# Rope products shifted on VectorE and the low parts of a head pair's weights formed on GpSimd, in a latent-attention kernel

## The reference, cut to what matters

```python
q = jnp.einsum('bsr,rhd->bshd', q_c, w_uq)
q_nope, q_rope = q[..., :MLA_NOPE], q[..., MLA_NOPE:]
q_rope = apply_rope(q_rope, cos[:, :, None, :], sin[:, :, None, :])
k_rope = apply_rope(k_r, cos, sin)
...
def apply_rope(x, cos, sin):
    x1 = x[..., :half]; x2 = x[..., half:]
    return jnp.concatenate([x1 * cos - x2 * sin, x2 * cos + x1 * sin], axis=-1)
...
p = softmax over the keys of (q_nope k_nope + q_rope k_rope) * scale, masked
return (o * jax.nn.silu(z)) @ w_out
```

## Time and profile before

| what | value |
|---|---|
| median of 3 runs | 1910.67 us (1909.27 to 1917.45) |
| profiled execution, its own time | 1910.41 us |
| span of its trace | 1908.6 us |
| PE busy | 1826.2 us, 96% of the span |
| DVE, ACT, POOL busy | 43%, 38%, 42% |
| the 8 pairs of heads | 423.3 to 695.6 us |

### The profile page before, as it was taken

One profiled execution on the slowest core, in us unless ns is written; L12 is line 12 of the kernel. 1 busy time (PEld: TensorE's weight loads), 2 busy tenths in 40 slices (PEclk: granted clock), 3 DMA queues, 4 the chain that ended last, 5 costly groups with the idle time before them and its releaser, 6 DMA issues.

```text
span 1908.6 us, 24042 instructions
## 1 busy us (share of the span) xinstructions
PE 1826.2 (96%) x8812; PEld 1504.3 (79%) x8812; DVE 819.2 (43%) x1378; ACT 734.8 (38%) x1022; POOL 802.8 (42%) x998
## 2 busy tenths in 40 slices
PE   5999899989999999899999999999998999999998
PEld 5887778877777778788888888888965788888886
DVE  7478666467666660732151111101668351111102
ACT  2223322264555551422254434322546454344222
POOL 1566565345000044246515555443434135555442
PEclk9999999999999999999999999999999999999999
DMA  9234645421111223233324334332320223333331
GB/s 306 89 111 132 187 155 194 143 62 58 49 58 36 68 89 110 67 88 110 109 68 110 88 101 115 104 110 89 101 70 29 61 73 104 88 106 91 103 107 66
DMA packets 211648, 191.19 MB, mean 100 GB/s; under 512 B 10503, under 2 KB 192890, under 8 KB 211578
## 3 DMA queue, kind: packets, MB, share of 16 engines
q1 hardware_dynamic: 210944, 189.95, 32.2%
q10 hardware_dynamic: 634, 0.29, 0.1%
HBM read 188.12 MB, written 2.10 MB: 100 GB/s over the span
## 4 chain that ended last, share of the span: by engine, by line
PE 79%; DVE 9%; ACT 4%; issue 3%; POOL 2%; DMA 1%; SPq 1%; DVEq 0%; ACTq 0%; POOLq 0%
PE PS L1668 24%; PE PS L1670 24%; PE PS L1669 24%; PE PS L1964 2%; ACT w_high L693 1%; PE PS L1796 1%; POOL w_low L607 1%; DVE soft L1430 1%; ACT probs L870 1%; SPq L433 1%; DVE ada_odd L1085 1%; DMA ada_raw<-in_ada_w 1%; PE PS L1995 1%; POOL w_low L635 1%; DVE q_rope_parts L1417 1%
## 5 line engine op out<-in xcount | busy, mean ns | idle before, releaser
L607 POOL TENSOR_TENSOR w_low<-w_raw,w_high 128x256 fp32r<-128x256 f32 x949 | 741.1, 817 | 1033.1 <-ACT w_high L693 1032.9
L1668 PE MATMUL PS<-h_high,w_high 128*128 128x512 f32 (+1 forms) x1488 | 559.5, 376 | 15.9 <-DVE h_low L1328 7.0
L693 ACT ACTIVATE w_high<-w_raw 128x2048 fp32r<-128x2048 f32 (+1 forms) x150 | 281.9, 1879 | 726.9 <-PE PS L1670 691.4
L1670 PE MATMUL PS<-h_high,w_low 128*128 128x512 f32 (+1 forms) x1488 | 554.7, 373 | 0.0
L1669 PE MATMUL PS<-h_low,w_high 128*128 128x512 f32 (+1 forms) x1488 | 554.7, 373 | 0.0
L1668 PEld LDWEIGHTS PS<-h_high,w_high 128*128 128x128 f32 x1488 | 282.4, 190 | 68.7 <-DVE h_low L1328 8.3
L1670 PEld LDWEIGHTS PS<-h_high,w_low 128*128 128x128 f32 x1488 | 282.2, 190 | 49.1
L1669 PEld LDWEIGHTS PS<-h_low,w_high 128*128 128x128 f32 x1488 | 282.4, 190 | 46.0 <-issue 0.5
L1257 DVE TENSOR_TENSOR w_low<-w_raw,w_high 128x2048 fp32r<-128x2048 f32 x18 | 41.3, 2292 | 338.5 <-ACT w_high L693 338.5
L1202 DVE TENSOR_TENSOR gate_buf<-gate_buf,PS 128x512 f32<-128x512 f32 x44 | 30.3, 688 | 335.0 <-ACT gate_buf L743 334.3
L1668 PE MATMUL PS<-w_high,ff_high 128*128 128x512 f32 x352 | 137.3, 390 | 0.1
(11 more groups left out here) (302 smaller groups left out, 2562.5 us busy)
## 6 DMA issues: line engine op xcount, KB each, us to landing
w_raw<-in_f_gate_up SPq DMA_DIRECT2D x88, 512.0 KB, 4.9
w_raw<-in_e_w_in SPq DMA_DIRECT2D x40, 512.0 KB, 5.1
w_raw<-in_f_down SPq DMA_DIRECT2D x40, 512.0 KB, 4.2
gains<-in_ada_w SPq DMA_DIRECT2D x16, 1024.0 KB, 5.2
w_raw<-in_a_w_in SPq DMA_DIRECT2D x24, 512.0 KB, 4.4
w_raw<-in_o_w_in SPq DMA_DIRECT2D x20, 512.0 KB, 4.4
ada_raw<-in_ada_w SPq DMA_DIRECT2D x8, 1024.0 KB, 11.8
w_raw<-in_e_w_out SPq DMA_DIRECT2D x16, 512.0 KB, 6.5
```

The costliest lines, as they stand in the source:

```text
L607: ins = nc.gpsimd.tensor_tensor(WL[s][:, piece], raw[s][:, piece], WH[s][:, piece].bitcast(F32), ALU.subtract)
L693: nact(WH[s][:, 0:n], raw[s][:, 0:n], ACT.Copy).then_inc(w_high[s], 1)
L1668: mm(dst, lh, rh, start=first, stop=False, skip_group_check=True)
L1670: return mm(dst, ll, rh, start=False, stop=last, skip_group_check=True)
```

## The change

1. **Rope.** TensorE's turn of the rope queries and ScalarE's copy `q_raw` go. VectorE multiplies the rope queries from PSUM by the cosine (128x512), then four blocks of 32 rows from PSUM by the sine, each written to its partner's rows of `q_part`, and adds (`rotated`). The sine table carries the sign of the row that is read (`sign_col`, one more small VectorE instruction while the tables are made). The rope queries of the next pair come right after its queries (`rope_of`), in PSUM bank 4, and their rotation stands at the end of VectorE's pair.
2. **Low parts.** For pairs 1 to 7 GpSimd forms all of slot 0's low part (5 pieces of 256) and columns 768 to 2047 of slot 1's (5 pieces); VectorE forms columns 0 to 767. GpSimd takes slot 0 of pair 1 after `affine`.
3. **Pair order.** `project` holds the keys alone (banks 1 and 5); the values move to after `score(3)`. ScalarE, not VectorE, copies the values out of PSUM. The gates of pair i-1 are multiplied after unit 1 of pair i. The second head's key and rope low parts move behind unit 1. ScalarE writes slot 0's high part at unit 3 (before: unit 0) and the next queries' high part before the Silu. `Z` starts with 4 steps of z, not 3.
4. **Before the first pair** the 4 matmuls of the gate rows go between the third and fourth tile of the latent transposes, and `gate_keep` ahead of `qcL`.

```diff
                 if name == "mla":
...
+                    with pool.Fori(1, 8) as j:
+                        low(j, 0, MLA_CHUNK)
+                        pool.wait_ge(w_high[1], j + (B.split[1] + 1))
+                        for c in range(Z_DVE, CHUNK, SLICE):
+                            piece = slice(c, c + SLICE)
+                            ins = nc.gpsimd.tensor_tensor(WL[1][:, piece], raw[1][:, piece], WH[1][:, piece].bitcast(F32), ALU.subtract)
+                        ins.then_inc(z_pool, 1)
+                        pool.wait_ge(z_pool, j)
+                        pool.wait_ge(z_dve, j)
+                        pool.sem_inc(w_split[1], 1)
+                        pool.sem_inc(raw_free[1], 1)
...
-                act.wait_ge(proj_done, i * 4 + 2)
-                nact(qraw[:, :], PS[:, 0, :], ACT.Copy).then_inc(qa_ready, 1)
                 act.wait_ge(proj_done, i * 4 + 3)
-                nact(knH[:, :, :], PS[:, 4:6, :], ACT.Copy).then_inc(kn_high, 1)
+                for h in range(2):
+                    nact(knH[:, h, :], PS[:, 1 + 4 * h, :], ACT.Copy).then_inc(kn_high, 1)
...
-                    if u == 0:
+                    if u == 2:
+                        act.wait_ge(proj_done, i * 4 + 4)
+                        nact(vh[:, :, :], PS[:, 6:8, :].rearrange("p a (b n) -> p (a b) n", b=2), ACT.Copy).then_inc(kv_ready, 1)
+                    if u == 3:
                         split_high(*(("mla", i + 1) if more else ("oout", 0)), 0)
                 act.wait_ge(used[1], B.use[1] + i + 1)
                 if more:
                     split_high("mla", i + 1, 1)
+                    queries_high(i + 1)
...
+            def rotated(dst, bank):
+
+                v.tensor_tensor(dst[:, :], PS[:, bank, :], cosM[:, :], ALU.mult)
+                half = ROPE // 2
+                for r in range(0, P, half):
+                    to = r + half if r % ROPE == 0 else r - half
+                    ins = v.tensor_tensor(q_part[to:to + half, :], PS[r:r + half, bank, :], sinM[r:r + half, :], ALU.mult)
+                steps.link(ins)
+                return v.tensor_tensor(dst[:, :], dst[:, :], q_part[:, :], ALU.add)
...
                 norm(0)
                 norm(1)
-                v.tensor_copy(vh[:, :, :], PS[:, 6:8, :].rearrange("p a (b n) -> p (a b) n", b=2)).then_inc(kv_ready, 1)
+                keys_low(1)
+                rope_low(1)
+                if not first:
+                    gate_heads(i - 1)
...
                 if more:
-                    split_low("mla", i + 1, 1)
+                    dve.wait_ge(w_high[1], i + (BASE["mla"].split[1] + 2))
+                    v.tensor_tensor(WL[1][:, 0:Z_DVE], raw[1][:, 0:Z_DVE], WH[1][:, 0:Z_DVE].bitcast(F32), ALU.subtract).then_inc(z_dve, 1)
...
+                    rope_queries(i + 1)
...
-                Z = (0, 3, 6, 8, 10, 12, 14, 15, 15, 16, 16)
+                Z = (0, 4, 7, 9, 10, 12, 14, 15, 15, 16, 16)
                 z_parts(0, Z[1])
+                pe.wait_ge(kr_ready, 1)
                 pe.wait_ge(qr_ready, i * 2 + 1)
                 score(0)
+                z_parts(Z[1], Z[1] + 1)
                 pe.wait_ge(qn_ready, i + 1)
                 score(1)
-                z_parts(Z[1], Z[2])
+                z_parts(Z[1] + 1, Z[2])
...
+                    if u == 1:
+                        values_of(i)
...
             with pe.Fori(0, 7) as i:
                 attend(i)
                 queries_of(i + 1)
+                pe.wait_ge(pT_ready, i * 8 + 7)
+                rope_of(i + 1)
                 weigh(i, 1)
                 project(i + 1)
```

More of the change, by code:

```diff
@@ L155, in constants @@
         low = (m % ROPE) < half
-        turn_m[m + half if low else m - half, m] = -1.0 if low else 1.0
+        turn_m[m + half if low else m - half, m] = -1.0
+    sign_col = np.where((r % ROPE) < half, 1.0, -1.0)[:, None].astype(np.float32)
     rot, rh = HD // 4, HD // 8
@@ L895, in attend @@
                 nact(oz[:, 2 * i:2 * i + 2, :], PS[:, 0:2, :], ACT.Silu).then_inc(sz_ready, 1)
-                if more:
-                    queries_high(i + 1)
             queries_high(0)
@@ L1371, in _ @@
                 ins.then_inc(latn_ready, 1)
+            gate_keep(1, 0)
             for j in range(2):
@@ L1377, in _ @@
             ins.then_inc(lat_low, 1)
-            gate_keep(1, 2)
             dve.wait_ge(lat_ev, 4)
@@ L1404, in gate_head, with rope_queries, gate_heads, attend @@
                 v.tensor_tensor(oz[:, i * 2 + h, :], PS[:, 6 + h, :], oz[:, i * 2 + h, :], ALU.mult).then_inc(oz_ready, 1)
-            def attend(i, more):
-                dve.wait_ge(qa_ready, i * 2 + 2)
-                steps.link(v.tensor_tensor(qr[:, :], qraw[:, :], cosM[:, :], ALU.mult))
-                dve.wait_ge(q_turn, i + 1)
-                steps.link(v.tensor_tensor(qraw[:, :], PS[:, 1, :], sinM[:, :], ALU.mult))
-                v.tensor_tensor(qr[:, :], qr[:, :], qraw[:, :], ALU.add).then_inc(qr_sum, 1)
-                dve.wait_ge(kn_high, i + 1)
-                for h, r in enumerate(HEAD_ROWS):
-                    v.tensor_tensor(knL[:, h, :], PS[:, 4 + h, :], knH[:, h, :].bitcast(F32), ALU.subtract)
+            def rope_queries(i):
+                dve.wait_ge(proj_done, i * 4 + 2)
+                rotated(qr, 4).then_inc(qr_sum, 1)
+            def gate_heads(i):
+                dve.wait_ge(sz_ready, i + 1 + CREDIT)
+                gate_head(i, 0)
+                gate_head(i, 1)
+            def attend(i, first, more):
+                def keys_low(h):
+                    dve.wait_ge(kn_high, i * 2 + h + 1)
+                    v.tensor_tensor(knL[:, h, :], PS[:, 1 + 4 * h, :], knH[:, h, :].bitcast(F32), ALU.subtract)
+                def rope_low(h):
+                    r = HEAD_ROWS[h]
                     dve.wait_ge(qr_high, i * 2 + h + 1)
                     v.tensor_tensor(qrHL[HEAD_ROWS[1 - h], h, :], qr[r, :], qrHL[r, h, :].bitcast(F32), ALU.subtract).then_inc(qr_ready, 1)
-                    if h == 0:
-                        v.tensor_tensor(qnL[:, 1, :], PS[:, 3, :], qnH[:, 1, :].bitcast(F32), ALU.subtract).then_inc(qn_ready, 1)
-                dve.wait_ge(proj_done, i * 4 + 4)
-                dve.sem_inc(used[0], 1)
+                keys_low(0)
+                rope_low(0)
+                v.tensor_tensor(qnL[:, 1, :], PS[:, 3, :], qnH[:, 1, :].bitcast(F32), ALU.subtract).then_inc(qn_ready, 1)
                 def top(u):
@@ L1459, in attend @@
                     low_o(1)
-                dve.wait_ge(sz_ready, i + 1 + CREDIT)
-                gate_head(i, 0)
+                    gate_heads(i)
                 if more:
                     queries_low(i + 1)
-                gate_head(i, 1)
+                    rope_queries(i + 1)
             queries_low(0)
-            with dve.Fori(0, 7) as i:
-                steps.loop(i, 2 + 8 * 3)
-                attend(i, True)
+            rope_queries(0)
+            steps.loop(0, 1 + 8 * 3)
+            attend(0, True, True)
+            steps.n = steps.first
+            with dve.Fori(1, 7) as i:
+                steps.loop(i, 1 + 8 * 3)
+                attend(i, False, True)
             steps.done(7)
-            attend(7, False)
+            attend(7, False, False)
             dve.wait_ge(oz_ready, HEADS + CREDIT)
```

49 lines of the change are left out of this document (24 added, 25 removed).

## The result

The changed kernel takes 1904.23 us (median of 7 runs, 1901.73 to 1905.67); the kernel before, run beside it, 1913.01. The measured ratio is 0.9949 with a 95% interval of 0.9934 to 0.9963 (the quotient of the two medians is 0.9954): faster by 0.5%. The profiled execution's span is 1903.4 us, 5.2 less than before.

What follows compares the result with a forecast made beforehand. TensorE, busy 96% of the span, was taken as the bound. Stall +2.2, clock +1.7, steady pairs -10.4 and last pair -0.6 sum to -7.1: 1903.5 us against the median, with an 8-in-10 range of 1897.0 to 1909.5.

Steps and rivals of the forecast that it cites:

- A steady pair without any wait takes 31.12: TensorE in a steady pair: the last pair's 31.99 less the turn's 0.87, so at most 2.5 gained from 33.63.
- The narrow product costs what a wide one does: VectorE's 32-row sine products of the rope queries: 0.69 us each, as fewer rows don't shorten a product.
- The edge costs 0.1: Where one pair meets the next: TensorE's keys wait about 0.1 us for ScalarE's later Silu, with no reserve left.
- Two softmax products lose 0.2 to 0.3 each beside GpSimd, together 0.5: Softmax, around units 6 and 7: GpSimd's slot-0 pieces slow two VectorE products, adding 0.5 us a pair.
- VectorE's chain equals TensorE's: Softmax stretch of a steady pair: VectorE's chain 18.4 us against TensorE's 18.3 of work.
- Five steady pairs: Steady pairs go from 33.63 to 31.9, a gain of 1.73 each; the prediction counted six, 10.4 us.
- Other work before the first pair: net 0: Before the first pair: gate rows fill an idle 1.2, transposes end 0.5 later, `gate_keep` is done sooner; net 0.
- The second pair starts 2.2 later: Second pair's start: TensorE idles 3.8 us for GpSimd's slot 0 low part after `affine`, arriving 2.2 us later.
- The low clock costs 1.7: After the 3.8 us wait before the second pair: 1.2 GHz level for about 3.3 us, half lost, 1.7.
- The last pair gains 0.6: Last pair, already without pieces: gains the turn's 0.87 less some 0.3 of new meetings, 0.6 us.
- nothing waits: Rival: steady pairs at 31.2, no half clock after the stall, 1897.4 us; chance 0.29 together with one of the two.
- The softmax chain becomes the bound: Rival: two products a pair lose a whole piece, narrow products or later Silu cost half a microsecond; 32.9, 1910; chance 0.12.

## Why the prediction came out right

The median, 1904.23, is 0.7 over the forecast. That it is so close is luck: the forecast was 1910.67 - 7.1, while the medians differ by 8.8, from the 1913.01 of seven runs. "Faster by more than 0.5%", where the result lies, just so, had a chance of 0.32. The kinds of cost and their places were right, and two errors of size, at the stall with its clock and at the steady pairs, both made the gain larger than forecast. The profiled region's account, with the steps as I put them:

- *A steady pair without any wait takes 31.12.* The pairs without the collision took 31.25, and the turn's 0.87 measured 0.89 when it was put back. The number is right, its working is not. The last pair's 31.99 ends where its last `turn` starts (the row below), while the steady pair's 33.63 holds that `turn` too, 0.41 by starts (525.02 to 525.43). With it the last pair takes 32.40, the steady pair is 1.23 longer and not 1.64, and 32.40 - 0.87 is 31.53. No run says where the other 0.28 came from, so this hit is partly luck.

```profile
692.00 0.63 PE L1995 MATMUL PS<-small,probs 128*128 128x128 f32 x4
```

- *The narrow product costs what a wide one does.* 0.687 against the 0.69 taken. Right.
- *The edge costs 0.1.* It has no bracketed wait; the keys wait 0.17 for the Silu. The rope queries' sum ends 538.46, 8.9 into the pair, as worked out, and its low part at 10.46 against 10.5. The cover ahead of the first score is 0.2, and both orders that moved that chain back cost 1.7 a pair.
- *Two softmax products lose 0.2 to 0.3 each beside GpSimd, together 0.5.* The sum is right, by luck, the split isn't: unit 6's product loses 0.56 (0.98 against 0.42), and unit 7's (528.59) comes after the pieces have ended (527.79). With it the pair is 31.77 against 31.9.
- *VectorE's chain equals TensorE's.* It does, within some 0.2 us. A copy of 1.22 put into it made unit 7's product 1.03 later and cost 0.93 against the pair without the collision. So the 0.56 of the collision comes through nearly whole, and it is the one thing that a steady pair still visibly waits for.
- *Five steady pairs* then gave 5 x 1.73 = 8.7 by the forecast. They gave 168.2 - 158.3 = 9.9, 0.5 of it in the one pair without the collision.
- *Other work before the first pair: net 0.* The stretch from the latents' transposes to the first pair's queries shrank from 6.79 to 6.05 (423.31 - 416.52 and 427.79 - 421.74). This 0.74 is a gain that the forecast put at nothing; no run undoes the moves in it, so which of them gives it is open.
- *The second pair starts 2.2 later.* From the latents' transposes it starts 1.3 later (42.94 against 41.63 us). The 2.05 by which the first pair grew is what I forecast, and the 0.74 is off it. The direction and the releaser are right, but TensorE waited 1.98, not 3.8. Slot 0's low part was ready 42.9 behind the latents' transposes, 0.9 sooner than by the forecast (460.3 - 416.52 = 43.8). And TensorE had lost time ahead of that: in the changed kernel's first pair the windows from 436.16 have the clock at 0.61 and 0.82 behind the wait for slot 1, and 0.55 us were waited at the last `turn`. The low clock in the first pair so ate a part of the stall. In the run with the turn product put back the clock was 1.00 there, and the wait was 4.06.
- *The low clock costs 1.7.* 1.33 was all that the second pair took over a steady one, and the queries' pace assigns 1.37 to the clock.
- *The last pair gains 0.6.* It gained 0.2 (35.55 to 35.32). GpSimd's pieces for the output projection now fall on units 6 and 7, whose products take 0.75 and 0.85 (0.42 and 0.49 before, when they fell on units 4 and 5, with 0.71 and 0.56), and the last `turn` waits 0.60 for VectorE, which before it didn't:

```profile
687.84 0.63 PE L2031 MATMUL PS<-small,probs 128*128 128x128 f32 x4 [0.60 <-DVE probs L1468]
```

In sum +1.3 -0.55 (the second pair: 1.33 of clock less 1.88 of a steady pair's gain) -9.9 -0.2 = -9.4 in the region, where -7.1 was forecast. The stall and its clock cost 2.6 instead of 3.9, five steady pairs gave 1.2 more, the last 0.4 less, and the second's steady gain was 0.15 more. The span fell by 5.2 and the medians by 8.8; the region started 5.2 us later in that execution (421.74 against 416.52), in code that the change touches only by one product, for the sign of the sines. In the eleven other executions of the changed code there it started anywhere between 416.9 and 421.9, so I take it for scatter; of the kernel before there is one profile, which can't show that.

Of the rivals, "nothing waits" came true for one pair in three of the executions, and for no more. "The softmax chain becomes the bound" needed two products to lose a piece each; one did, nearly whole (0.56 of 0.72). The Trainium skill ("SBUF — State Buffer", section "Who interferes with whom") has VectorE's scalar product, in a two-port mode, blocked for GpSimd's whole instruction if it comes second; the trace of the changed kernel is nearer to that than the average of 0.2 that I had read from the earlier trace rows.

## What to carry to other kernels

When work moves to an idle engine, ask what that engine is doing at the first turn of the loop: GpSimd was idle in the steady pairs, but at `affine` ahead of the second, and taking the pieces before the last block of it gave back 3.4 us of the first two pairs. Price a wait on TensorE at its length plus what the clock does behind it. Measure a reserve at the consumer itself, by the end of its last producer, not from another run's wait. And where an experiment shifts a chain, look whether it also shifts what the chain collides with, before its length is read as a price: the values' copy looked half as dear as it was.

## What was not expected of the hardware

- **Who loses a collision changes.** Beside the same five GpSimd pieces the same 384-column product took 0.98 in most pairs, and 0.42 in one (GpSimd then 3.70, not 3.60). By the Trainium skill ("SBUF — State Buffer", "Who interferes with whom") the order of issue decides which of the two is blocked; this trace agrees in that the two paid in turn, though GpSimd's price was 0.10 and VectorE's 0.56. The two outcomes lie hundredths of a microsecond apart: in the changed kernel VectorE's product began 1.34 us behind the start of the pieces where it lost, and 1.32 where GpSimd did; at 1.17, with the values' copy on VectorE, it took 0.47 and GpSimd 3.60.
- **The clock behind a wait.** Like waits had unlike ends. With the Silu first, each steady pair waits 1.62 to 1.80 us for `q_rope_parts`. Behind the wait that ends at 546.53 (1.63) the clock stayed at 1.00; behind the one that ends at 613.42 (1.62) it fell, and the pair took 34.55 instead of 33.45:

```profile
547.00:550.00 3.00, 3.00 (x18) 2.37 (x18) 1.80 (x9) 1.61 (x5) 0.00 (x0) 1.00 0.00 0
...
613.40:616.40 3.00, 2.98 (x14) 2.75 (x15) 1.24 (x4) 1.61 (x3) 0.00 (x0) 0.67 0.01 3
616.40:619.40 3.00, 3.00 (x13) 2.48 (x13) 2.59 (x9) 0.84 (x3) 0.00 (x0) 0.76 0.00 0
```

Behind a wait of 1.98 the low clock lasted three microseconds in one execution and six in another. Behind the first pair's wait of 2.33 for slot 1 it was 0.61 and 0.82 in the changed kernel and 1.00 in the run with two unused products. What decides it stays open; no run here told it.
